# Splitting half a chunk earlier in the FFN turns, a reordered norm, and a later request for the norm's vectors

## The chip, the cores and the metric

The kernel runs on one core of a Trainium2 chip. TensorE (PE) multiplies, VectorE (DVE) and ScalarE (ACT) work beside it, GpSimd (POOL) does small work, and SyncE (SP) issues the loads from HBM in a program of its own. The metric is the device time of one execution in microseconds, lower is better: 3050.05 us before, the median of 3 runs (3048.78 to 3052.07).

## The reference

Two layers over a stream x of 256 tokens by 2048 channels, everything in float32:

```
proj = x @ w_in + b_in                       # 2048 -> 3*1024 + 512 + 512 + 3*2048
p_sb = stick_breaking_attention(q, k, v) @ sb_w_out
p_ssm = glu(gelu(s5(u))) @ ssm_w_out
p_mem = memory_attention(q_mem, mem) @ mem_w_out
merged = sum of sigmoid(gate_b) * p_b
x = layer_norm(ALPHA * x + merged @ w_o) * ln1_g + ln1_b
gate, up = split(x @ ffn_w_gate_up)          # 2048 -> 2 * 5632
x = layer_norm(ALPHA * x + (silu(gate) * up) @ ffn_w_down) * ln2_g + ln2_b
```

The change touches the first norm of each layer, the FFN behind it, and a few steps of the second norm of the first layer.

## The kernel before

**Numbers.** Each float32 operand is split into two parts: hi is a copy rounded to the type fp32r, lo is the rest. A product is hi times hi, hi times lo and lo times hi. The activations xs hold both parts of x side by side (columns 0 to 255 hi, 256 to 511 lo).

**Chunks.** All weights come in chunks of 1 MB (128 partitions by 2048) into one of 4 slots of `raw`. A chunk is split in two halves of 128x1024. For each half ACT writes the hi part (`hi_half`, L631, one ACTIVATE), and DVE subtracts it to get lo (`lo_half`, L978, one TENSOR_TENSOR). There are 4 buffers for halves, so half h of chunk c+2 can be split only when PE has finished half h of chunk c (semaphore `half_done`). The helper `split_next` at chunk c splits both halves of chunk c+1. PE waits on `lo_ready` before each half (L1481 and L1483 for gate/up, L1491 to L1493 for the rows of the down projection, L1466 and L1469 for other products).

**Each engine's instructions are written out by hand** and run in that order; between engines stand semaphores alone. An instruction that waits holds everything behind it on its engine.

**An FFN turn** has 12 chunks: 0 to 7 gate/up, two for each of four pairs of tiles (q = 0 to 3: gate, up, gate, up), 8 to 11 down. There are 11 turns in a layer: the first, nine in a loop, the last. After each odd chunk c < 8 comes the eviction of its pair: ACT waits for the whole chunk, copies the PSUM part to `pt` (L929), DVE adds (L1424, into gg or uu). For an up pair (c = 3 and c = 7) DVE then multiplies twice (L1428, L1432), ACT writes the hi of `hT` (L936) and DVE its lo (L1435). In program order the split of chunk c+1 stands before the eviction, the split of chunk c+2 after it.

**The norm** after w_o (v = 0 in layer 0, v = 2 in layer 1; `which` = 0) and the one after the FFN (`which` = 1). DVE gathers the statistics and the scale `rv` (L1037 to L1063), both engines centre the rows in five pieces (0 to 127, 128 to 511, then three of 512; DVE token half 0 at L1071, ACT half 1 at L711). PE transposes 16 slices (L1560, `turn(k)`, two instructions each), the two engines apply g and b in turn (DVE L1078 even k, ACT L718 odd k), ACT writes the hi part (L726), DVE the lo part (L1083), and PE multiplies slice k at once (`step(k)`: for `which` = 0 the first pair of the FFN, chunks 0 and 1). turn(k) for k of 4 to 7 needs the third piece centred. 16 matmuls that nobody reads, "fillers" (L1836), stand on PE between w_o and the first norm.

**Loads.** SP issues chunk after chunk; the request for a chunk waits until the lo parts of the chunk 4 before it are done (L368). The vectors ln_g and ln_b are broadcast into `gbh` in two parts of 1024 columns, 512 KB each vector (L455, `load_norm`); a request for the second part waits for `resid_done`, which DVE raises in the first FFN turn after two of four residual steps (L1115 and L1119, at c = 2 and c = 4; the other two, at c = 6 and c = 8, use the second part).

Of the kernel before, what the change touches and what calls it, by code (L numbers as in the profile page):

```python
# [19 lines left out]
KD = D // P  # L20
# [93 lines left out]
def trunk(nc, x, mem, w_in, b_in, sb_w_out, lam_re_d, lam_im_d, log_dt_d, b_re_d, b_im_d, c_re_d,  # L114
# [3 lines left out]
    with ctx:  # L118
# [234 lines left out]
        def _(sp):  # L353
# [29 lines left out]
            for l in range(DEPTH):  # L383
# [85 lines left out]

                def ffn_loads(i, first=False):  # L470
                    for c in range(8):
                        if first and c == 7:
                            load_norm(2 * l, 1)
                        load("FF", l, i, c, column_pair(w_gu[l], i * 512 + (D_FF * ((c // 2) % 2) + 256 * (c // 4)),
                                                        8 * (c % 2)))
                    for c in range(4):
                        load("FF", l, i, 8 + c, block_rows(w_down[l], bass.ds(i * 4 + 2 * (c % 2), 2),
                                                           1024 * (c // 2)))
# [144 lines left out]
        def _(act):  # L623
# [35 lines left out]
            def done(ph, l, i, c, h=1):  # L659
                return chunk_no(ph, l, i, c) * 2 + (h + 1 + HALF_CREDIT)  # L660
# [41 lines left out]
            def norm(l, which):  # L702

                v = 2 * l + which
                ph, i, c = ("U", 0, 0) if which else ("FF", 0, 0)

                def centre(q):
                    y = rows[:, 1, CENTRES[q]:CENTRES[q + 1]]
                    if q == 0:
                        act.wait_ge(ln_step, LN_STEPS * (v + 1))  # L710
                    act.activation(y, y, ACT.Identity, bias=rv[:, 4, 1:2], scale=rv[:, 1, 1:2]).then_inc(norm_act, 1)  # L711

                def affine(k):
                    g, b = norm_cols(l, which, k)
                    act.wait_ge(ln_T, 16 * v + k + 1)
                    if k >= 4:
                        act.wait_ge(xs_lo, 16 * v + k - 3)
                    act.activation(xf[:, k % 4, :], bank[k % 4][:, 0:T], ACT.Identity, bias=b, scale=g  # L718
                                   ).then_inc(aff_act, 1)

                def hi_part(k):
                    if k % 2:
                        act.wait_ge(aff_act, 8 * v + k // 2 + 1)
                    else:
                        act.wait_ge(aff_dve, 8 * v + k // 2 + 1)
                    act.activation(xs[:, k, 0:T], xf[:, k % 4, :], ACT.Copy).then_inc(xs_hi, 1)  # L726

                split_next(ph, l + which, i, c)
                centre(0)
                centre(1)  # L730
                for k in range(0, KD, 2):
                    affine(k + 1)
                    hi_part(k)
                    hi_part(k + 1)
                    if k in (0, 2, 4):
                        centre(2 + k // 2)

            for l in range(DEPTH):

# [176 lines left out]
                def ffn_turn(i, first, last):  # L916
                    n = i + 11 * l
                    for c in range(12):
                        if last and c == 11:
                            if not last_l:  # L920
                                for h in range(2):
                                    hi_half("U", l + 1, 0, 0, h)
                        elif not (first and c == 0):
                            split_next("FF", l, i, c)
                        if c < 8 and c % 2:
                            q, a = c // 2, c // 4
                            act.wait_ge(half_done, done("FF", l, i, c))
                            act.wait_ge(tile_out, tile_no("FF", l, i, q) + 1)
                            act.activation(pt[:, q % 2], banks[:, PAIR_BANK[q]:PAIR_BANK[q] + 2, 0:T], ACT.Copy  # L929
                                           ).then_inc(first_out, 1)  # L930
                            if q % 2 == 0:
                                act.wait_ge(tile_out, tile_no("FF", l, i, q) + (1 + TILE_CREDIT))
                                act.activation(th[:], gg[:], ACT.Tanh, scale=0.5).then_inc(ffn_th, 1)
                            else:
                                act.wait_ge(ffn_step, n * 4 + (2 * a + 2 + 2))
                                act.activation(hT[:, 2 * a:2 * a + 2, 0:T], hh[:], ACT.Copy).then_inc(ffn_hi, 1)  # L936
# [17 lines left out]
        def _(dve):  # L954
# [70 lines left out]
            def norm(l, which):  # L1025
                v = 2 * l + which
                base = LN_STEPS * v
                k = [0]
# [57 lines left out]
                def split(h):  # L1086
                    lo_half(PHASES[nxt[0]][1][nxt[3]], hl_slot(ph, c + 1, h), h,
                            chunk_no(ph, l + which, i, c) * 2 + (2 + h))

                centre(0)  # L1090
                centre(1)
                affine(0)
# [3 lines left out]
                for k in range(2, KD, 2):  # L1096
                    affine(k)
                    lo_part(k - 2)
                    lo_part(k - 1)
                    if k < 6:  # L1100
                        centre(2 + k // 2)
                    if k == 4 and not which:
                        split(0)
                    if k == 8:
                        split(1)
                lo_part(KD - 2)
                lo_part(KD - 1)

            def residual(v, q):

# [41 lines left out]
            for l in range(DEPTH):  # L1152
# [245 lines left out]

                def ffn_turn(i, first, last):
                    n = i + 11 * l  # L1400
                    for c in range(12):
                        if last and c == 11:
                            if not last_l:
                                for h in range(2):
                                    lo_half(PHASES["U"][1][0], h, h, chunk_no("U", l + 1, 0, 0) * 2 + h)
                        elif not (first and c == 0) and not (last and c == 10):
                            split_next("FF", l, i, c)
                        if last and c == 9:
                            row = [(m, 0, banks[:, 4 + 2 * m:6 + 2 * m, :],
# [9 lines left out]
                        if c < 8 and c % 2:  # L1419
                            q, a = c // 2, c // 4  # L1420
                            src = banks[:, PAIR_BANK[q]:PAIR_BANK[q] + 2, T:2 * T]
                            dve.wait_ge(ffn_step, n * 4 + (2 * a + 1 + q % 2))
                            dve.wait_ge(first_out, tile_no("FF", l, i, q) + 1)
                            dve.tensor_tensor((gg, uu)[q % 2][:], pt[:, q % 2], src, ALU.add).then_inc(tile_out, 1)  # L1424
# [33 lines left out]
        def _(pe):  # L1458
# [88 lines left out]
            def norm(l, which, step):  # L1547
# [16 lines left out]
                for k in range(4):  # L1564
                    turn(k)
                for k in range(KD):
                    if k + 4 < KD:
                        turn(k + 4)
                    pe.wait_ge(xs_lo, 16 * v + k + 1)
                    step(k)  # L1570

            for l in range(DEPTH):

# [258 lines left out]
                    pair_k("FF", l, 0, k // 8, k, PAIR_BANK[0], k == KD - 1)  # L1832

                pe.wait_ge(rows_out, sums_no("WO", l, 1, 0))
                for k in range(16):
                    pe.matmul(bank[0], ident_r[:], xs[:, k, :], start=True, stop=True)  # L1836
                norm(l, 0, first_pair)
                for q in range(1, 4):
                    ffn_pair(0, q)
# [52 lines left out]
```

## Time and profile before

| | us |
|---|---|
| median of 3 runs | 3050.05 |
| the profiled execution, its time | 3046.98 |
| its span | 3045.2 |
| PE busy | 2973.9 (98%) |
| DVE busy | 2055.1 (67%) |
| ACT busy | 1455.0 (48%) |
| mean share of the DMA engines on the weight queue | 59.3% |

PE is busy almost always. The other engines have room on average, so what costs time are the places where PE waits for one of them at that moment. "Busy" is drawn a little long for PE: matmuls overlap, and the row of one reaches beyond the start of the next.

### The profile page before, as it was taken

What the parts mean: (1) busy time and instruction counts of PE and PEld (TensorE: products, weight loads), DVE (VectorE), ACT (ScalarE), POOL (GpSimd) and SP (SyncE); (2) the same over time, 40 slices, a digit from 0 to 9 for tenths busy, and PEclk for the clock granted to TensorE, in tenths of its full rate; (3) what the DMA queues carried; (4) which work ended last, traced back from release to release, by engine and by line L of the source; (5) the groups of instructions that cost most, each with busy time, mean ns of one, the idle gap of its engine ahead of it and who ended that gap; (6) DMA issues with size and microseconds to landing.
All of it is one profiled execution on the core that took longest, in us unless ns stands there. A gap on an engine that the chain in (4) does not pass through costs nothing.

```text
span 3045.2 us, 46770 instructions
## 1 busy us (share of the span) xinstructions
PE 2973.9 (98%) x16206; PEld 2538.1 (83%) x16206; DVE 2055.1 (67%) x3163; ACT 1455.0 (48%) x1975; POOL 130.2 (4%) x191
## 2 busy tenths in 40 slices
PE   6999999999999999999999999999999999999999
PEld 5888888888788888888878888888878888888887
DVE  5999766665765555555699996666667556555656
ACT  4556555554444444444455655555444444444443
POOL 5000011110000000000000000000000000000000
PEclk8999999999999999999999999999999999999999
DMA  8656577675555555555465656767755555555554
GB/s 276 164 155 170 153 193 192 180 206 207 202 186 192 193 191 179 181 193 191 161 161 159 163 158 180 200 174 197 231 177 180 193 184 174 192 193 180 190 183 151
DMA packets 672969, 562.16 MB, mean 185 GB/s; under 512 B 20760, under 2 KB 637568, under 8 KB 671872
## 3 DMA queue, kind: packets, MB, share of 16 engines
q1 hardware_dynamic: 668688, 548.48, 59.3%
q10 hardware_dynamic: 4208, 12.74, 1.1%
q8 instruction: 43, 0.70, 0.1%
q14 instruction: 30, 0.25, 0.0%
HBM read 552.78 MB, written 8.39 MB: 184 GB/s over the span
## 4 chain that ended last, share of the span: by engine, by line
PE 82%; DVE 10%; ACT 3%; issue 3%; POOL 1%; DMA 1%; ACTq 1%; DVEq 0%; POOLq 0%
PE banks L1466 21%; PE banks L1481 19%; PE banks L1469 11%; PE banks L1483 9%; PE banks L1491 6%; PE banks L1493 5%; PE banks L1492 5%; DVE lo L978 3%; PE banks L1757 2%; ACT hi L631 2%; DVE hh L1432 1%; DVE hh L1428 1%; PE banks L1759 1%; ACT pt L929 1%; DVE st L1139 1%
## 5 line engine op out<-in xcount | busy, mean ns | idle before, releaser
L978 DVE TENSOR_TENSOR lo<-raw,hi 128x1024 fp32r<-128x1024 f32 x1016 | 1214.5, 1238 | 262.6 <-ACT hi L631 230.5
L631 ACT ACTIVATE hi<-raw 128x1024 fp32r<-128x1024 f32 x884 | 890.0, 1051 | 352.2 <-PE banks L1493 235.9
L1481 PE MATMUL banks<-xs,hi 128*128 128x512 f32 x2816 | 892.1, 398 | 10.9 <-DVE lo L978 10.5
L1466 PE MATMUL banks<-xs,hi 128*128 128x512 f32 x2544 | 807.0, 399 | 6.0 <-DVE lo L978 4.7
L1483 PEld LDWEIGHTS banks<-xs,lo 128*128 128x128 f32 x2816 | 530.7, 188 | 125.4
L1469 PEld LDWEIGHTS banks<-xs,lo 128*128 128x128 f32 x2544 | 478.7, 188 | 113.2
L1483 PE MATMUL banks<-xs,lo 128*128 128x256 f32 x2816 | 555.0, 279 | 0.0
L1469 PE MATMUL banks<-xs,lo 128*128 128x256 f32 x2544 | 500.9, 278 | 0.0
L1481 PEld LDWEIGHTS banks<-xs,hi 128*128 128x128 f32 x2816 | 432.0, 189 | 17.6 <-DVE lo L978 16.0
L1466 PEld LDWEIGHTS banks<-xs,hi 128*128 128x128 f32 x2544 | 388.7, 189 | 14.0 <-issue 7.4
L1491 PE MATMUL banks<-hi,hT 128*128 128x512 f32 x704 | 276.4, 393 | 8.4 <-DVE lo L978 8.4
L1492 PE MATMUL banks<-lo,hT 128*128 128x512 f32 x704 | 274.2, 389 | 0.0
L1493 PE MATMUL banks<-hi,hT 128*128 128x512 f32 x704 | 274.1, 389 | 0.0
L929 ACT ACTIVATE pt<-banks 128x512 f32<-128x512 f32 x88 | 52.8, 600 | 387.0 <-PE banks L1483 387.0
L656 ACT ACTIVATE tmp<-banks,par 128x256 f32<-128x256 f32 x144 | 68.4, 475 | 326.8 <-PE banks L1469 326.8
L1128 DVE TENSOR_TENSOR rows<-rows,banks 128x1024 f32<-128x1024 f32 (+1 forms) x98 | 109.5, 1152 | 108.7 <-PE banks L1493 108.6
L643 ACT ACTIVATE hi<-raw 128x1024 fp32r<-128x1024 f32 x132 | 134.8, 1052 | 79.6 <-PE banks L1493 79.6
L1491 PEld LDWEIGHTS banks<-hi,hT 128*128 128x128 f32 x704 | 132.1, 188 | 43.7 <-DVE lo L978 14.8
L1493 PEld LDWEIGHTS banks<-hi,hT 128*128 128x128 f32 x704 | 132.1, 188 | 27.8
L1492 PEld LDWEIGHTS banks<-lo,hT 128*128 128x128 f32 x704 | 132.2, 188 | 26.0
L1424 DVE TENSOR_TENSOR uu<-pt,banks 128x512 f32<-128x512 f32 x44 | 30.3, 688 | 165.2 <-ACT pt L929 165.2
L1424 DVE TENSOR_TENSOR gg<-pt,banks 128x512 f32<-128x512 f32 x44 | 30.3, 688 | 144.6 <-ACT pt L929 144.6
(216 smaller groups left out, 2683.3 us busy)
## 6 DMA issues: line engine op xcount, KB each, us to landing
raw<-in_ffn_w_gate_up SPq DMA_DIRECT2D x176, 1024.0 KB, 5.1
raw<-in_w_in SPq DMA_DIRECT2D x160, 1024.0 KB, 7.6
raw<-in_ffn_w_down SPq DMA_DIRECT2D x88, 1024.0 KB, 5.2
raw<-in_w_o SPq DMA_DIRECT2D x32, 1024.0 KB, 5.3
raw<-in_mem_w_kv SPq DMA_DIRECT2D x16, 1024.0 KB, 5.5
raw<-in_sb_w_out SPq DMA_DIRECT2D x32, 512.0 KB, 4.1
raw<-in_ssm_w_out SPq DMA_DIRECT2D x32, 256.0 KB, 4.4
raw<-in_mem_w_out SPq DMA_DIRECT2D x32, 256.0 KB, 4.8
```

The costliest lines, as they stand in the source:

```text
L631: act.activation(hi[:, hl_slot(ph, c, h), :], raw[:, slot, h * HALF:(h + 1) * HALF], ACT.Copy).then_inc(hi_ready, 1)
L643: act.activation(hi[:, hl_slot(ph, c + 1, h), :], raw[:, slot, h * HALF:(h + 1) * HALF], ACT.Copy).then_inc(hi_ready, 1)
L929: act.activation(pt[:, q % 2], banks[:, PAIR_BANK[q]:PAIR_BANK[q] + 2, 0:T], ACT.Copy).then_inc(first_out, 1)
L978: dve.tensor_tensor(lo[:, s, :], raw[:, slot, h * HALF:(h + 1) * HALF], hi[:, s, :].bitcast(F32), ALU.subtract).then_inc(lo_ready, 1)
L1128: dve.tensor_tensor(y2, y2, src, ALU.add).then_inc(rows_out, 1)
L1466: pe.matmul(dst[:, :], hi[:, s, k * P:(k + 1) * P], x_t[:, k0 + k, :], start=first and k == 0, stop=False)
L1469: ins = pe.matmul(dst[:, 0:T], lo[:, s, k * P:(k + 1) * P], x_t[:, k0 + k, 0:T], start=False, stop=last and k == 7)
L1481: pe.matmul(bank[base + j], hi[:, s, at[j]], xs[:, k, :], start=k == 0, stop=False)
L1483: ins = pe.matmul(bank[base + j][:, 0:T], lo[:, s, at[j]], xs[:, k, 0:T], start=False, stop=last)
L1491: pe.matmul(dst, xh, hi[:, s, w], start=first, stop=False)
L1492: pe.matmul(dst, xh, lo[:, s, w], start=False, stop=False)
L1493: return pe.matmul(dst, xl, hi[:, s, w], start=False, stop=last)
```

## The change

1. In an FFN turn, half 0 of chunk c+2 is split ahead of the eviction after c = 1, 3, 5, 7; half 1 follows in the next step of the loop (c in 2, 4, 6, 8).
2. In the first norm of a layer ACT also splits chunk 2, half 0 after slice 10 and half 1 after slice 14, and DVE follows (`second_pair`). So the first turn doesn't split chunk 2 any more.
3. ACT in both norms: the third piece is centred and the hi part of slice 0 written before ACT's first `affine`.
4. PE in the first norm: 24 fillers for 16, and turn(4) behind step(0).
5. SP: ln_g and ln_b, second part, are requested behind gate/up chunk 7 of the first turn, not ahead of it.

```diff
@@ ffn_loads
                     for c in range(8):
-                        if first and c == 7:
-                            load_norm(2 * l, 1)
                         load("FF", l, i, c, column_pair(...))
+                    if first:
+                        load_norm(2 * l, 1)
@@ norm, scalar
                 centre(0)
                 centre(1)
+                centre(2)
+                hi_part(0)
                 for k in range(0, KD, 2):
                     affine(k + 1)
-                    hi_part(k)
+                    if k:
+                        hi_part(k)
                     hi_part(k + 1)
-                    if k in (0, 2, 4):
+                    if k in (2, 4):
                         centre(2 + k // 2)
+                    if k in (10, 14) and not which:
+                        hi_half("FF", l, 0, 2, (k - 10) // 4)
@@ ffn_turn, scalar (vector: the same with lo_ahead)
-                        elif not (first and c == 0):
+                        elif c in (2, 4, 6, 8):
+                            hi_half("FF", l, i, c + 1, 1)
+                        elif not (first and c < 2):
                             split_next("FF", l, i, c)
                         if c < 8 and c % 2:
                             q, a = c // 2, c // 4
+                            hi_half("FF", l, i, c + 2, 0)
                             act.wait_ge(half_done, done("FF", l, i, c))
@@ norm, vector
+                    if k == 12 and not which:
+                        second_pair(0)
                 lo_part(KD - 2)
                 lo_part(KD - 1)
+                if not which:
+                    second_pair(1)
@@ norm, tensor
                 for k in range(KD):
-                    if k + 4 < KD:
+                    if k + 4 < KD and (k or which):
                         turn(k + 4)
                     pe.wait_ge(xs_lo, 16 * v + k + 1)
                     step(k)
+                    if k == 0 and not which:
+                        turn(4)
@@ tensor, fillers
-                for k in range(16):
-                    pe.matmul(bank[0], ident_r[:], xs[:, k, :], start=True, stop=True)
+                for k in range(24):
+                    pe.matmul(bank[0], ident_r[:], xs[:, k % KD, :], start=True, stop=True)
```

ScalarE in the loop over FFN turns, from chunk 2's split to the eviction of the up pair. The kernel before (`hi` a half's hi part, `pt` the copy from PSUM, `hT` the hi part of the down projection's input, raw_full the arrival of a chunk in slot 0 to 3):

```order
L929 ACTIVATE pt<-banks 128x512 [waits tile_out]
L932 REGISTER_ALU
L933 ACTIVATE th<-gg 128x512 [waits tile_out]
L629 REGISTER_ALU
L630 ISA [waits raw_full3]
L631 ACTIVATE hi<-raw 128x1024 [waits half_done]
L630 REGISTER_ALU
L631 ACTIVATE hi<-raw 128x1024 [waits half_done]
L629 REGISTER_ALU
L630 ISA [waits raw_full0]
L631 ACTIVATE hi<-raw 128x1024 [waits half_done]
```

The changed kernel, at the same place:

```order
L630 ISA [waits raw_full3]
L631 ACTIVATE hi<-raw 128x1024 [waits half_done]
L935 REGISTER_ALU
L936 ISA [waits half_done]
L937 ACTIVATE pt<-banks 128x512 [waits tile_out]
L940 REGISTER_ALU
L941 ACTIVATE th<-gg 128x512 [waits tile_out]
L630 REGISTER_ALU
L631 ACTIVATE hi<-raw 128x1024 [waits half_done]
L629 REGISTER_ALU
L630 ISA [waits raw_full0]
```

The wait for chunk 3's arrival and its first hi part moved from behind `pt` and `th` to ahead of them; the second hi part stayed behind. The same happens at c = 3, 5 and 7, and on DVE.

PE at the start of the first norm, before (`ident_r` marks the fillers, `ident,rows` a transpose, `xs,hi` and `xs,lo` a step):

```order
L1836 MATMUL banks<-xs,ident_r 128x512 x15
L1560 MATMUL banks<-ident,rows 128x128 [waits norm_act,norm_done]
...
L1560 MATMUL banks<-ident,rows 128x128 [waits aff_dve,norm_act,norm_done]
L1560 MATMUL banks<-ident,rows 128x128
L1481 MATMUL banks<-xs,hi 128x512 [waits lo_ready,rows_out,xs_lo]
L1481 MATMUL banks<-xs,hi 128x512
L1483 MATMUL banks<-xs,lo 128x256 x2
```

And now:

```order
L1860 MATMUL banks<-xs,ident_r 128x512 x23
L1582 MATMUL banks<-ident,rows 128x128 [waits norm_act,norm_done]
...
L1503 MATMUL banks<-xs,hi 128x512 [waits lo_ready,rows_out,xs_lo]
L1503 MATMUL banks<-xs,hi 128x512
L1505 MATMUL banks<-xs,lo 128x256 x2
L1582 MATMUL banks<-ident,rows 128x128 [waits aff_dve,norm_act,norm_done]
L1582 MATMUL banks<-ident,rows 128x128
```

Eight fillers more, and the transpose that waits for DVE's first `affine` and for the third centred piece moved behind the first step.

SP in the first FFN turn, before (the end of w_o, seven gate/up chunks, the vectors, the eighth chunk, the down chunks):

```order
L368 DMA raw<-in_w_o 128x2x1024 [waits lo_ready] x5
L368 DMA raw<-in_ffn_w_gate_up 128x8x256 [waits lo_ready] x7
L455 DMA gbh<-in_ln_g 128x1024 [waits resid_done]
L455 DMA gbh<-in_ln_b 128x1024
L368 DMA raw<-in_ffn_w_gate_up 128x8x256 [waits lo_ready]
L368 DMA raw<-in_ffn_w_down 128x2x1024 [waits lo_ready] x4
```

And now, the same stretch of SP:

```order
L368 DMA raw<-in_w_o 128x2x1024 [waits lo_ready] x5
L368 DMA raw<-in_ffn_w_gate_up 128x8x256 [waits lo_ready] x8
L455 DMA gbh<-in_ln_g 128x1024 [waits resid_done]
L455 DMA gbh<-in_ln_b 128x1024
L368 DMA raw<-in_ffn_w_down 128x2x1024 [waits lo_ready] x4
```

The wait for `resid_done` now holds back the four down chunks and not the eighth gate/up chunk.

## Rows read from the trace of the kernel before

**Rows 1.** The page's first line.
```profile
span 3045.2 us, 46770 instructions
```
**Rows 2.** PE's waits, whole run: engine line waited for: us in total, times, longest us.
```profile
PE banks L1481 <- DVE lo L978: 10.5, 20, 3.4
PE banks L1491 <- DVE lo L978: 10.0, 24, 0.8
```
**Rows 3.** Timeline, PE, chunk 5 of a loop turn: start, us, line, xcount, [idle before <-releaser].
```profile
1223.82 0.62 PE L1481 MATMUL banks<-xs,hi 128*128 128x512 f32 x2
1224.51 0.63 PE L1481 MATMUL banks<-xs,hi 128*128 128x512 f32 x2
...
1225.58 0.73 PE L1481 MATMUL banks<-xs,hi 128*128 128x512 f32 x2 [0.21 <-DVE lo L978]
```
**Rows 4.** Timeline, ACT and DVE, the same place.
```profile
1219.91 0.60 ACT L929 ACTIVATE pt<-banks 128x512 f32<-128x512 f32 x1 [4.59 <-PE banks L1483]
...
1224.30 4.63 DVE L978 TENSOR_TENSOR lo<-raw,hi 128x1024 fp32r<-128x1024 f32 x4 [0.26 <-ACT hi L631]
```
**Rows 5.** Timeline, chunk 9 of the same turn: the eviction on ACT, then PE.
```profile
1242.69 0.60 ACT L929 ACTIVATE pt<-banks 128x512 f32<-128x512 f32 x1 [4.59 <-PE banks L1483]
...
1248.43 0.50 PE L1491 MATMUL banks<-hi,hT 128*128 128x512 f32 x1 [0.40 <-DVE lo L978]
```
**Rows 6.** Timeline, first turn of layer 0: PE at chunks 7 and 9.
```profile
831.68 0.50 PE L1481 MATMUL banks<-xs,hi 128*128 128x512 f32 x1 [3.36 <-DVE lo L978]
...
843.28 0.47 PE L1491 MATMUL banks<-hi,hT 128*128 128x512 f32 x1 [0.30 <-DVE lo L978]
```
**Rows 7.** Timeline, first turn of layer 0: DVE, SP and ACT around the vectors' request.
```profile
803.13 2.36 DVE L978 TENSOR_TENSOR lo<-raw,hi 128x1024 fp32r<-128x1024 f32 x2 [1.65 <-ACT hi L631]
...
820.41 0.34 SPq L455 DMA_DIRECT2D gbh<-in_ln_g  x1
...
821.27 0.43 SPq L368 DMA_DIRECT2D raw<-in_ffn_w_gate_up  x1
...
829.31 2.00 ACT L631 ACTIVATE hi<-raw 128x1024 fp32r<-128x1024 f32 x2 [4.47 <-DMA raw<-in_ffn_w_gate_up]
```
**Rows 8.** Timeline, PE, first norm of layer 0.
```profile
774.09 3.89 PE L1836 MATMUL banks<-xs,ident_r 128*128 128x512 f32 x16
780.07 0.41 PE L1560 MATMUL banks<-ident,rows 128*128 128x128 f32 x2 [2.09 <-ACT rows L711]
...
783.41 1.20 PE L1481 MATMUL banks<-xs,hi 128*128 128x512 f32 x2
...
789.62 0.71 PE L1481 MATMUL banks<-xs,hi 128*128 128x512 f32 x2
...
799.80 0.73 PE L1481 MATMUL banks<-xs,hi 128*128 128x512 f32 x2
```
**Rows 9.** Stretches: us, PE, PEld, DVE, ACT, POOL busy, granted clock, DMA share, GB/s.
```profile
782.00:783.00 1.00, 0.00 (x0) 0.00 (x0) 0.98 (x3) 1.00 (x3) 0.00 (x0) 0.54 1.14 492
...
1543.00:1544.00 1.00, 0.00 (x0) 0.00 (x0) 1.00 (x3) 1.00 (x4) 0.00 (x0) 1.00 0.00 0
```
**Rows 10.** Timeline, DVE and ACT, first norm of layer 0.
```profile
782.02 0.76 DVE L1083 TENSOR_TENSOR xs<-xf,xs 128x256 fp32r<-128x256 f32 x2
...
782.20 0.80 ACT L711 ACTIVATE rows<-rows,rv 128x512 f32<-128x512 f32 x1
```
**Rows 11.** Timeline, PE, second norm of layer 0: last product before, first and last step.
```profile
1540.13 0.39 PE L1469 MATMUL banks<-mT,lo 128*128 128x256 f32 x2
...
1544.57 0.50 PE L1587 MATMUL banks<-xs,hi 128*128 128x512 f32 x1
...
1555.24 0.28 PE L1588 MATMUL banks<-xs,lo 128*128 128x256 f32 x1
```
**Rows 12.** SP in a loop turn: chunk 9's request; time to landing, requests of 1214 to 1240.
```profile
1226.83 0.37 SPq L368 DMA_DIRECT2D raw<-in_ffn_w_down  x1
...
DMA to landing us min/median/max: 5.0/5.2/6.5
```

More of the change, by code:

```diff
@@ L1088, in split, with second_pair @@
                             chunk_no(ph, l + which, i, c) * 2 + (2 + h))
+                def second_pair(h):
+                    lo_half(PHASES["FF"][1][2], hl_slot("FF", 2, h), h, chunk_no("FF", l, 0, 2) * 2 + h)
                 centre(0)
@@ L1400, in ffn_turn, with lo_ahead @@
                     n = i + 11 * l
+                    def lo_ahead(c, h):
+                        lo_half(PHASES["FF"][1][c], hl_slot("FF", c, h), h, chunk_no("FF", l, i, c) * 2 + h)
                     for c in range(12):
@@ L1405, in ffn_turn @@
                                     lo_half(PHASES["U"][1][0], h, h, chunk_no("U", l + 1, 0, 0) * 2 + h)
-                        elif not (first and c == 0) and not (last and c == 10):
+                        elif c in (2, 4, 6, 8):
+                            lo_ahead(c + 1, 1)
+                        elif not (first and c < 2) and not (last and c == 10):
                             split_next("FF", l, i, c)
@@ L1421, in ffn_turn @@
                             src = banks[:, PAIR_BANK[q]:PAIR_BANK[q] + 2, T:2 * T]
+                            lo_ahead(c + 2, 0)
                             dve.wait_ge(ffn_step, n * 4 + (2 * a + 1 + q % 2))
```

## The prediction

> **What bounds the kernel now.** First the page: the span is 3045.2 us [rows 1] and PE is busy 98% of it, so a gain can only come from what PE still waits for, or from steps it does at half clock. So the second view is PE's waits over the whole run [rows 2]. Two lines matter to this change: gate/up matmuls waited for a lo part 20 times, 10.5 us in all, one wait of 3.4 us; down matmuls 24 times, 10.0 us. The third view is the timeline at such places, to see the chain that ends late.
>
> In a turn of the loop PE comes to chunk 5 at 1225.58. A pair of matmuls and its partner take 0.69 to 0.70 us (1223.82 to 1224.51), so without a wait it would have come at 1225.21: 0.37 us are lost, of which the view shows 0.21 as idle, since each row is drawn some 0.16 us beyond the next start [rows 3]. What it waited for: the eviction begins at 1219.91, five steps on ACT and DVE follow, and only then does DVE start chunk 5's first lo part at 1224.30, ending 1225.5 [rows 4]. It was late for one reason: its hi part stands behind the eviction in ACT's order, though its buffer was free half a chunk before. At chunk 9 the same, after the eviction that begins at 1242.69: 0.40 idle and the same 0.16, so 0.56 us [rows 5].
>
> In the first turn of a layer PE waits 3.36 us at chunk 7 (3.52 lost) and 0.30 at chunk 9 (0.46 lost) [rows 6]. The first is a load: chunk 3's lo parts were done at 805.5, from then on chunk 7 could have been requested, but SP stood at the request for ln_g, which waits for the second residual step on DVE; it left at 820.41, chunk 7 at 821.27, and ACT got it at 829.31 after waiting 4.47 us [rows 7].
>
> In the first norm PE has its fillers at 774.09, then waits 2.09 us for the first transpose at 780.07; the first step comes at 783.41, the fifth at 789.62, chunk 2 at 799.80 [rows 8]. Four steps in 6.21 us are slow: the granted clock fell within 782 to 783 (0.54 in that stretch), the lower of its two levels, 1.2 GHz [rows 9]. From 789.62 on, eight steps with a transpose and four without (0.70 each) take 10.18 us, so one with a transpose takes 0.92.
>
> **The change part by part.** *A half ahead of the eviction.* hi of chunk c+2, half 0, needs PE to be through chunk c, half 0, which is 2.8 us before the eviction can begin. So hi (1.06) and lo (1.23) are ready about when the eviction starts, over 5 us before PE needs them. Nothing is added: the same ACTIVATE and TENSOR_TENSOR, elsewhere. What is late next is half 1. It stays behind the eviction, but moves into half 0's place: its lo ends at 1225.5 instead of 1226.7, and PE needs it at 1225.21 + 2.79 = 1228.0, so 2.5 us are left. For chunk 9 likewise: 1248.4 against 1247.9 + 2.7, 2.2 us left. The ahead split adds a wait on ACT: for the arrival of chunk c+2, with the eviction queued behind it. Chunk 9 is the tightest: requested at 1226.83, landing 5.0 to 6.5 us later [rows 12], by 1233.3; ACT turns to it 2.8 us ahead of the eviction, at about 1239.8. So I count all of it gone. Nine loop turns in two layers: 18 x (0.37 + 0.56) = 16.7 us. First and last turn of each layer, chunk 9 alone: 4 x 0.46 = 1.8 (the last turn taken as the first). Their chunk 5 shows no wait in the view; up to 1.1 more may hide there, which I leave out.
>
> *The vectors behind chunk 7.* Its request moves from 821.27 to about 805.5, lands by 812 and is needed at 828. 2 x 3.52 = 7.0 us. What is now behind SP's wait are the four down chunks. Chunk 8 used to come fourth behind the two vectors and chunk 7; now it takes chunk 7's place, on ACT at 829.3 at the latest, lo at 831.6, and PE wants it at 828.2 + 5.6 = 833.7: 2.1 us are left, more since the second residual step now stands behind one lo part and not two. The residual steps that use the vectors get them no later.
>
> *The norm.* Fillers: 16 take 3.73 us to the next start, 24 take 5.6 and end at 779.7; the transposes start at 780.07 whatever they do, so they cost nothing, with 0.4 us to spare. First step: it needed turn(4), which waited for ACT's third centred piece, 782.20 to 783.0; it now needs only slice 0's lo part. DVE's first two ran from 782.02, the first ends at 782.4 [rows 10]. hi of slice 0 can't be later than before: its input is ready at 781.1 and the centred piece takes about 0.5. So the first step comes at 782.45, 0.95 us earlier. The clock: in the second norm PE's last full product ended at 1540.4 and the first step came at 1544.57, 4.2 us with only transposes between [rows 11], and the granted clock stayed 1.00 [rows 9]. In the first norm it was 777.8 to 783.41, 5.6 us, and it fell. With 24 fillers and the earlier step it is 779.7 to 782.45, 2.8 us. So I take the upper level, 2.4 GHz: 12 x 0.92 + 4 x 0.70 = 13.8 us from 782.45, chunk 2 at 796.3, 3.5 us gained if PE alone sets the pace.
>
> The Trainium skill, "TensorE: Matmul & The Clock Gate", Part 4: PE-mode transpose, says that a transpose doesn't count as PE being busy in the way a matmul does. That speaks against counting only the idle pieces (0.4 and 0.95 us) as quiet, and it is why I compare the whole stretches; by either count the changed norm is quieter for less time than the second norm, which kept its clock. It raises my chance of a fall from 3 to 8 in 100, and doesn't change the sum.
>
> DVE and ACT have to keep up. In the second norm, paced by them, 16 steps took 1544.57 to about 1555.4, 10.8 us [rows 11]; chunk 2's first lo part adds 1.2. 12.0 is under 13.8, so in total they can, but the split halves (1.2 us each) stand between slices and will make single steps late. Bounds per norm: 3.5 (none late) and 1.0 (clock falls: 0.95, little else). I take 2.6, nearer to the upper one since the sum of DVE's work fits. 2 x 2.6 = 5.2. The reordering in the second norm I count at nothing: DVE sets the pace there, and its order is as before.
>
> Sum: 16.7 + 1.8 + 7.0 + 5.2 = 30.7 us. The profiled execution took 3046.98 us (span 3045.2), so 3016.3 there; the median before, 3050.05, lies 3.1 above it. Predicted on that scale: 3019.3 us.
>
> **The rivals.** *The clock falls all the same.* For it: idle pieces remain. Against: the second norm. Each norm gains 1.0: 3022.5 us.
>
> *Half 1 takes the place of half 0.* For it: the eviction's chain is as long as before. Against: 2.2 to 2.5 us of margin. If half of the gain of the turns came back: 3019.3 + 9 = 3028 us.
>
> *The down chunks are late in the first turn.* They now queue behind the vectors; in the first turn before, queued requests took 8 us to arrive. Margin 2.1 us; if it is missed by as much as chunk 7 was, the 7.0 us return at chunk 8: 3026 us.
>
> *Slower than before: ACT holds the eviction for a load.* The place is c = 7 of each turn, hi of chunk 9 ahead of `pt`. If the landing took over some 16 us from 1226.83, the eviction would start late; its chain takes 4.1 us (1219.91 to 1224.04, where DVE's idle 0.26 begins [rows 4]), so it ends at 1246.8, and PE needs hT's second pair at 1247.9, so it decides from about 17 us on. At 20 us it would cost 3 us a turn, 66 us for 22 turns against 31 gained: 3085 us. Against it: 6.5 us is the longest landing in that stretch.
>
> *Nothing gained:* the waits only move to other places of the turn, 3050 us. The period of PE's work leaves no place I can name.
>
> **How the numbers follow.** Forecast 75 in 100, clock 8, half 1 5, down chunks 7, slower 3, nothing gained 2. The forecast's own range: the norm term from 1.0 to 3.5 each, the hidden 1.1, and some 2 us of spread of a median give 3014 to 3025. Holding the down chunks' and half 1's cases too, 3013 to 3028. Faster by over 0.2% (6 us, what a measurement of this kernel can tell): 0.95; within it 0.02; slower 0.03.
>
> **What would show it.** PE's waits: gate/up behind a lo part down from 20 to at most a few and none of 3 us; down matmuls behind a lo part without the 22 of the turns. A loop turn, 67.5 us before, takes 66.6. Clock 1.00 through the first norms, first step 2.8 us after the fillers, chunk 2 some 22.2 us after their start (25.7 before). Chunk 7 requested before the vectors. Wrong would make it: an ACT wait for a DMA inside the turns, a stretch at 0.50 clock in a first norm, a new PE wait at chunk 8, or steps of the norm more than 1.5 us behind slices from DVE.

## The result, and the profile after

3011.98 us, the median of 4 runs (3008.55 to 3012.73), against 3051.06 us (3048.78 to 3053.14, 4 runs). The ratio is 0.987, with a 95% interval of 0.9858 to 0.9882: 39.1 us faster. Forecast were 30.7 us and a range whose fast end was 3013 us. The direction was right, the size was too small by a fifth of the measured gain, and the time lies 1.0 us below the range. The profiled execution took 3008.55 us against 3046.98, so 38.4 us can be taken apart in the traces.

The page's first line, and PE's waits over the whole run (line waited for: us in total, times, longest us):

```profile
span 3006.8 us, 46802 instructions
```
```profile
PE banks L1488 <- DVE lo L986: 8.8, 7, 2.1
...
PE banks L1503 <- DVE xs L1091: 2.9, 4, 0.8
...
PE banks L1513 <- DVE lo L986: 1.5, 2, 0.8
```

Gate/up matmuls (L1503) no longer wait for a lo part at all, down matmuls (L1513) twice and outside the FFN turns [rows 2]. In their place stand four waits of a norm's step for DVE, 2.9 us; L1488 is other products, as before.

Chunk 5 of a loop turn, timeline of PE in the changed kernel:

```profile
1209.90 0.63 PE L1503 MATMUL banks<-xs,hi 128*128 128x512 f32 x2
1210.37 0.39 PE L1505 MATMUL banks<-xs,lo 128*128 128x256 f32 x2
1210.60 0.62 PE L1503 MATMUL banks<-xs,hi 128*128 128x512 f32 x2
1211.07 0.40 PE L1505 MATMUL banks<-xs,lo 128*128 128x256 f32 x2
```

The boundary at 1210.60 can't be told from any other [rows 3]. The same place, ACT and DVE:

```profile
1202.44 1.06 ACT L631 ACTIVATE hi<-raw 128x1024 fp32r<-128x1024 f32 x1 [1.73 <-PE banks L1505]
1203.53 1.23 DVE L986 TENSOR_TENSOR lo<-raw,hi 128x1024 fp32r<-128x1024 f32 x1 [1.56 <-ACT hi L631]
1205.31 0.60 ACT L937 ACTIVATE pt<-banks 128x512 f32<-128x512 f32 x1 [1.80 <-PE banks L1505]
...
1209.69 3.50 DVE L986 TENSOR_TENSOR lo<-raw,hi 128x1024 fp32r<-128x1024 f32 x3 [0.26 <-ACT hi L631]
```

Half 0's lo part is done at 1204.8, before the eviction (`pt`) starts and 5.8 us before PE needs it at 1210.60; half 1's is done at 1210.9, 2.5 us before PE needs it. That is as forecast [rows 4].

The first turn of layer 0: SP and ACT (chunk 7 is the second of the two requests of the first row; the down chunks come behind the vectors).

```profile
795.75 4.98 SPq L368 DMA_DIRECT2D raw<-in_ffn_w_gate_up  x2
815.15 0.34 SPq L455 DMA_DIRECT2D gbh<-in_ln_g  x1
...
816.01 1.78 SPq L368 DMA_DIRECT2D raw<-in_ffn_w_down  x3
```
```profile
824.35 2.01 ACT L631 ACTIVATE hi<-raw 128x1024 fp32r<-128x1024 f32 x2 [3.07 <-DMA raw<-in_ffn_w_down]
826.90 1.06 ACT L631 ACTIVATE hi<-raw 128x1024 fp32r<-128x1024 f32 x1 [0.54 <-DMA raw<-in_ffn_w_down]
829.43 0.60 ACT L937 ACTIVATE pt<-banks 128x512 f32<-128x512 f32 x1 [1.47 <-PE banks L1505]
```

Chunk 7 is requested over 14 us ahead of the vectors, and nobody waits for it [rows 7]. ACT does wait for chunk 8 now, 3.07 us, and for chunk 9 ahead of an eviction, 0.54 us; but it then waits for PE once more (1.47 us before `pt`), so neither costs anything.

The first norm of layer 0, PE, and the granted clock (us, PE, PEld, DVE, ACT, POOL busy, clock, DMA share, GB/s):

```profile
778.43 0.41 PE L1582 MATMUL banks<-ident,rows 128*128 128x128 f32 x2 [0.23 <-ACT rows L711]
...
780.72 0.72 PE L1503 MATMUL banks<-xs,hi 128*128 128x512 f32 x2 [0.85 <-DVE xs L1091]
...
784.60 0.38 PE L1582 MATMUL banks<-ident,rows 128*128 128x128 f32 x2
785.59 0.73 PE L1503 MATMUL banks<-xs,hi 128*128 128x512 f32 x2 [0.61 <-DVE xs L1091]
```
```profile
780.00:781.00 1.00, 0.28 (x1) 0.28 (x2) 0.84 (x3) 0.97 (x3) 0.00 (x0) 1.00 1.21 524
781.00:782.00 1.00, 1.00 (x9) 0.92 (x9) 0.77 (x3) 1.00 (x4) 0.00 (x0) 1.00 1.14 492
```

The fillers start at 772.44, so the first step comes after 8.3 us (9.3 before) [rows 8]. The end of the norm is measured below by the first eviction (ACT's first `pt`), which waits for the last step: it begins 23.55 us after the fillers' start, 25.77 before. PE starts chunk 2 close to it, 0.20 us ahead of it here and 0.06 us before the change. The clock stays at 1.00 [rows 9]. But the fifth step, at 785.59, waits for DVE.

Where the 38.4 us lie, from starts of the same instruction in both traces:

| term | forecast | measured | how measured |
|---|---|---|---|
| 18 loop turns | 16.7 | 21.3 | 67.52 to 66.34 us a turn |
| two first turns | 0.9 + 7.0 | 9.7 | 71.26 to 66.45 and 71.33 to 66.43, first eviction to first eviction |
| two last turns | 0.9 | 1.9 | 0.39 + 0.56 each |
| two first norms | 5.2 | 4.4 | fillers to the first eviction, 25.77 to 23.55 and 25.72 to 23.54 |
| all else | 0 | 1.1 | fillers of layer 0 start 1.65 earlier; 0.55 lost between the layers |

The last row can't be put down to the change: in the 14 profiled executions of this study the fillers of layer 0 started anywhere from 772.4 to 776.0 us, and the stretch from the last down matmul of layer 0 to the fillers of layer 1 took 734.6 to 736.2 us with the old as with the new order of the norms. The norm's row has some luck in it too: in the eight first norms profiled with the old norm and 16 fillers (two in each of four executions), the first eviction came 24.8 to 26.1 us after the fillers' start.

### The profile page after: what moved, and what is told of

Read it like the earlier page. It is cut to its first block, busy times and chain, and to the rows that moved or that the text cites. A ratio compares the mean times of both kernels' runs of the same rounds, so it can differ in the third digit from the quotient of the medians.

```text
span 3006.8 us, 46802 instructions
## 1 busy us (share of the span) xinstructions
PE 2958.4 (98%) x16222; PEld 2536.1 (84%) x16222; DVE 2062.7 (69%) x3163; ACT 1468.9 (49%) x1975; POOL 129.8 (4%) x191
## 4 chain that ended last, share of the span: by engine, by line
PE 92%; DVE 5%; POOL 1%; ACT 1%; issue 1%; ACTq 0%; DMA 0%; DVEq 0%; POOLq 0%
PE banks L1488 22%; PE banks L1503 22%; PE banks L1491 11%; PE banks L1505 11%; PE banks L1513 7%; PE banks L1514 7%; PE banks L1515 7%; PE banks L1781 2%; DVE lo L986 1%; PE banks L1783 1%; DVE st L1154 1%; DVE scan_t L1230 0%; DVE rows L1143 0%; DVE blocks L1238 0%; POOL sc L317 0%
## 5 line engine op out<-in xcount | busy, mean ns | idle before, releaser
L631 ACT ACTIVATE hi<-raw 128x1024 fp32r<-128x1024 f32 x884 | 904.9, 1053 | 542.1 <-PE banks L1505 288.0
L1503 PE MATMUL banks<-xs,hi 128*128 128x512 f32 x2816 | 886.4, 396 | 2.9 <-DVE xs L1091 2.9
L1488 PE MATMUL banks<-xs,hi 128*128 128x512 f32 x2544 | 807.6, 399 | 6.6 <-DVE lo L986 4.7
L1503 PEld LDWEIGHTS banks<-xs,hi 128*128 128x128 f32 x2816 | 430.0, 189 | 5.7 <-DVE xs L1091 3.9
L1488 PEld LDWEIGHTS banks<-xs,hi 128*128 128x128 f32 x2544 | 388.9, 189 | 14.6 <-issue 8.2
L1513 PE MATMUL banks<-hi,hT 128*128 128x512 f32 x704 | 274.0, 389 | 0.0
L643 ACT ACTIVATE hi<-raw 128x1024 fp32r<-128x1024 f32 x132 | 134.8, 1052 | 79.6 <-PE banks L1515 79.6
L1513 PEld LDWEIGHTS banks<-hi,hT 128*128 128x128 f32 x704 | 132.1, 188 | 26.7
L999 DVE SCALAR_TENSOR_TENSOR gate<-banks,tmp 128x256 f32<-128x256 f32 x96 | 40.8, 425 | 126.6 <-ACT tmp L656 126.6
L1513 PE MATMUL banks<-hi,mT 128*128 128x512 f32 x256 | 99.9, 390 | 1.5 <-DVE lo L986 1.5
```

The lines of the kernel that those rows point to most:

```text
L631: act.activation(hi[:, hl_slot(ph, c, h), :], raw[:, slot, h * HALF:(h + 1) * HALF], ACT.Copy).then_inc(hi_ready, 1)
L643: act.activation(hi[:, hl_slot(ph, c + 1, h), :], raw[:, slot, h * HALF:(h + 1) * HALF], ACT.Copy).then_inc(hi_ready, 1)
L1488: pe.matmul(dst[:, :], hi[:, s, k * P:(k + 1) * P], x_t[:, k0 + k, :], start=first and k == 0, stop=False)
L1503: pe.matmul(bank[base + j], hi[:, s, at[j]], xs[:, k, :], start=k == 0, stop=False)
L1513: pe.matmul(dst, xh, hi[:, s, w], start=first, stop=False)
```

## The experiments

Times are compared with the kernel before on the same chip. The time of a turn is that from an eviction to the same one nine turns later, by nine. Spreads of a median are some 2 us, traces agree to 0.02 us in the turns, so mechanisms are read from the traces.

**Only the half ahead in the turns** (`turns_only`): the turns' part of the diff on the kernel before, chunk 2 still split by the first turn. ScalarE's edits (VectorE's are the same, with `lo_ahead`):

```diff
+                        elif c in (2, 4, 6, 8):
+                            hi_half("FF", l, i, c + 1, 1)
                         elif not (first and c == 0):
                             split_next("FF", l, i, c)
                         if c < 8 and c % 2:
                             q, a = c // 2, c // 4
+                            hi_half("FF", l, i, c + 2, 0)
```

> Only the turns' half ahead of each eviction, on the kernel before. Theory (a wait costs its gap and then 0.11 us more in the first matmuls behind it, which the prediction left out): a loop turn of 67.53 us becomes 66.35, 18 of them give 21.2 us; first and last turns give some 4 and 1.9 more, since the second residual step also comes one lo part earlier and with it chunk 7's request: about 27 us faster than before. Rival (the gap alone, 0.93 a turn; the rest of the surplus is from other parts of the change): 66.60 a turn, about 21 us.

3023.27 us against 3050.68, ratio 0.9913 (0.9896 to 0.9929), 27.4 us. A loop turn took 66.337 us in both layers: all of the 1.18 us come from this part, 0.25 more than the visible gaps. The first turn did not behave as expected: from first eviction to first eviction it took 70.83 and 70.78 us in the two layers, 1.0 us less in all where some 4 were expected. SP asked for the vectors 1.6 us earlier, counted from the first eviction, but ACT met chunk 7 at another place:

```profile
827.41 1.06 ACT L631 ACTIVATE hi<-raw 128x1024 fp32r<-128x1024 f32 x1 [10.37 <-DMA raw<-in_ffn_w_gate_up]
828.38 0.58 ACT L932 ACTIVATE pt<-banks 128x512 f32<-128x512 f32 x1
```

With half 0 ahead, the late chunk holds the eviction as well: the stall moves one eviction forward. First to fourth eviction take 36.94 us against 37.69 in layer 0, but 37.76 against 37.73 in layer 1. PE's wait at chunk 7 was of about one length in both, 2.70 and 2.65 us. In layer 0 the clock stayed at 1.00 and two short waits followed behind the late eviction (0.39 and 0.56 us); in layer 1 the clock fell to 0.50 and those two were absent. This is the slower rival's mechanism, in the one place where a load is late enough. It also makes the forecast time partly luck: the traces account for 24.8 us (span 3045.2 to 3020.4), of which 24.2 lie in the turns, and the other 2.6 of the 27.4 are explained by nothing in them.

**Only the later request** (`load_only`).

```diff
-                        if first and c == 7:
-                            load_norm(2 * l, 1)
+                    if first:
+                        load_norm(2 * l, 1)
```

> Only the later request for ln_g and ln_b, on the kernel before. Theory: PE's wait at chunk 7 of each first turn goes, 3.52 + 0.11 each, 7.3 us, and no new wait at chunk 8. Rival (the down chunks are late instead): a new wait at chunk 8 of up to 3.5 us, near 0 gained.

3040.88 us against 3050.68, ratio 0.9965 (0.9952 to 0.9977), 9.8 us, more than the 7.3 expected. In the trace first to fourth eviction take 34.09 us against 37.69, 3.6 a layer as expected, and PE has no wait at chunk 8. The next run suggests why the time gains more.

**Only 24 fillers** (`fill24_only`).

```diff
-                for k in range(16):
-                    pe.matmul(bank[0], ident_r[:], xs[:, k, :], start=True, stop=True)
+                for k in range(24):
+                    pe.matmul(bank[0], ident_r[:], xs[:, k % KD, :], start=True, stop=True)
```

> Only 24 fillers for 16, on the kernel before. Theory (the clock falls when too little happens on PE between the fillers' end and the first step): the stretch without matmuls of full width shrinks from 5.6 to 3.8 us, the clock stays at 1.00, four steps take 3.7 and not 6.2 us, 2 x 2.4 = 4.8 us faster. Rival (the reordering is what kept the clock): it falls as before, 0 us.

3047.10 us against 3050.68; the interval of the ratio, 0.9982 to 1.0002, contains no change. The norm gained what the theory says: clock 1.00, first eviction 23.36 us after the fillers' start in both layers, 2.4 a layer. But most of it was given back some 30 us later, at the wait for chunk 7 (columns as above):

```profile
782.00:783.00 1.00, 0.00 (x0) 0.00 (x0) 0.96 (x4) 1.00 (x3) 0.00 (x0) 1.00 1.21 524
828.00:829.00 1.00, 0.00 (x0) 0.00 (x0) 0.70 (x1) 1.00 (x2) 0.00 (x0) 1.00 1.04 414
829.00:830.00 1.00, 0.41 (x1) 0.42 (x2) 1.00 (x2) 0.43 (x2) 0.00 (x0) 0.55 1.03 414
830.00:831.00 1.00, 1.00 (x4) 0.81 (x4) 1.00 (x2) 1.00 (x2) 0.00 (x0) 0.50 1.01 401
```

After waits of 3.42 and 4.48 us the granted clock fell to the lower level, and the part from the third to the fourth eviction took 16.15 and 17.19 us, against 14.77 and 14.80: 3.8 us given back of the 4.8 gained. Of layer 1's 2.4 us, 1.1 are the longer wait itself, so the fall costs 1.3 us in either layer. In the profiled execution of the kernel before the clock stayed at 1.00 behind the same wait of 3.36 us, in both layers. So this wait costs 3.6 us, and 1.3 more where the clock falls. That it fell in both layers in most unprofiled runs of the kernel before would explain the surplus of `load_only` (7.2 + 2.6 = 9.8 us). It is not shown: of those runs only the mean granted clock is recorded, 0.992 to 0.994, which is too coarse to tell.

**ScalarE alone ahead** (`after_act_ahead`): the changed kernel, DVE makes both lo parts behind the eviction.

```diff
                         elif c in (2, 4, 6, 8):
+                            lo_ahead(c + 1, 0)
                             lo_ahead(c + 1, 1)
...
-                            lo_ahead(c + 2, 0)
```

> The changed kernel, but in the turns only ScalarE splits a half ahead; VectorE makes both lo parts behind the eviction. VectorE then starts chunk 5's lo right after hT's lo, 0.2 us earlier than in the kernel before. Theory (gap + 0.11 each): gaps of 0.17 and 0.36, a loop turn of 66.35 + 0.28 + 0.47 = 67.10 us, 15 us slower than the changed kernel over 20 turns. Rival (gap alone): 66.88 us a turn, 11 us slower.

3020.07 us against 3050.68, ratio 0.9903 (0.9887 to 0.9920). A turn took 66.831 us, 0.49 more than 66.337. By that figure alone the rival came nearer, but the expected 0.75 and 0.53 both rested on gaps that I had put too long. The trace gives the real ones (timeline of PE at chunk 5, then at chunk 9):

```profile
1147.04 0.39 PE L1505 MATMUL banks<-xs,lo 128*128 128x256 f32 x2
1147.29 0.73 PE L1503 MATMUL banks<-xs,hi 128*128 128x512 f32 x2
1147.86 0.40 PE L1505 MATMUL banks<-xs,lo 128*128 128x256 f32 x2
...
1169.35 0.39 PE L1515 MATMUL banks<-hi,hT 128*128 128x512 f32 x1
1169.79 0.50 PE L1513 MATMUL banks<-hi,hT 128*128 128x512 f32 x1
1170.13 0.39 PE L1514 MATMUL banks<-lo,hT 128*128 128x512 f32 x1
```

Chunk 5 starts 0.25 behind its neighbour where 0.23 is usual, a gap of 0.02. But the pair that starts there takes 0.57 to the next start and not 0.47. At chunk 9 the gap is 0.44 - 0.23 = 0.21, and the next start comes after 0.34 instead of 0.23. Gaps alone make 0.23 a turn; with 0.10 and 0.11 behind them 0.44, near the 0.49 measured. With the true gaps the theory holds and the rival falls: even a wait of 0.02 us costs 0.12.

**A longer eviction chain** (`before_long_chain`, `after_long_chain`): on the kernel before and on the changed one.

```diff
+                                act.activation(tmp[:], hh[:], ACT.Copy)
                                 act.activation(hT[:, 2 * a:2 * a + 2, 0:T], hh[:], ACT.Copy).then_inc(ffn_hi, 1)
```

> The kernel before with one more ScalarE copy of 128x512 (0.53 us, nobody reads it) in each up pair's eviction. Theory (gap plus a fixed 0.11): both gaps of a loop turn grow by 0.53, the matmul behind them still takes 0.11 more than the others, the turn takes 67.52 + 1.06 = 68.58 us. Rival (the extra grows with the wait): the surplus doubles, over 68.7 us.

> The changed kernel with the same extra copy. Theory (half 1 has 2.2 to 2.5 us to spare): the loop turn stays at 66.34 us. Rival (half 1 is nearly late, the change has no room): it grows, up to 67.4.

On the kernel before a turn took 68.556 us, 1.04 more (3075.57 us, one run). PE at chunk 5:

```profile
1166.35 0.39 PE L1484 MATMUL banks<-xs,lo 128*128 128x256 f32 x2
1167.46 0.73 PE L1482 MATMUL banks<-xs,hi 128*128 128x512 f32 x2 [0.72 <-DVE lo L979]
1168.03 0.40 PE L1484 MATMUL banks<-xs,lo 128*128 128x256 f32 x2
```

The gap is 0.88 now, and the pair behind it takes the same 0.57. With gaps of 0.02, 0.37 and 0.88 us the surplus behind them was 0.10 each time: it is fixed. The run's time rose by 23.6 us, more than the turns explain, since the clock fell at the wait for chunk 7 in both layers here (waits of 3.53 and 3.42 us). On the changed kernel the turn took 66.337 us to the last digit (3010.61 us, one run): half 1 has at least the 0.53 us to spare, as forecast.

**The norm's parts**, four edits of the changed kernel, one kernel each. `after_fill16` and `after_fill32`, other numbers of fillers:

```diff
-                for k in range(24):
+                for k in range(16):
```
```diff
-                for k in range(24):
+                for k in range(32):
```

`after_norm_order`, the old order on ScalarE and on PE:

```diff
-                centre(2)
-                hi_part(0)
...
-                    if k:
-                        hi_part(k)
+                    hi_part(k)
...
-                    if k in (2, 4):
+                    if k in (0, 2, 4):
...
-                    if k + 4 < KD and (k or which):
+                    if k + 4 < KD:
...
-                    if k == 0 and not which:
-                        turn(4)
```

`after_late_split`, VectorE's split of chunk 1, half 0, one pair of slices later:

```diff
-                    if k == 4 and not which:
+                    if k == 6 and not which:
```

> The changed kernel with 16 fillers. Theory (the fillers keep the clock, not the reordering): the stretch without full-width matmuls is 3.7 to 8.3 us after the fillers' start, 4.6 us; the clock falls in the first norms, chunk 2 starts 25 to 26 us after the fillers' start instead of 23.55, 4 us slower in all. Rival (the earlier first step is enough): clock 1.00, 23.55, no change.

> The changed kernel with the old order of the norm on ScalarE and of turn(4) on PE; fillers 24, chunk 2's split still inside. Theory (VectorE's split between slices sets the pace, the earlier first step is given back): chunk 2 at 23.3 to 23.6 us after the fillers' start, as now, no difference in the time. Rival (the prediction's account: 0.95 us a norm from the earlier first step): 24.4 us, 2 us slower.

> The changed kernel, VectorE splits chunk 1's half 0 after slice 5's lo part and not after slice 3's. Theory (that split is what makes a step of the norm late by 0.77 us): the wait goes, chunk 2 comes about 22.8 us after the fillers' start instead of 23.55, 1.5 us faster in all, too little for the time alone. Rival (VectorE's work is as much, a later step is late instead): 23.5.

> The changed kernel with 32 fillers. Theory (fillers are free up to the first transpose at 5.98 us after their start): they end at 7.5 us, the first step comes 1.5 us later, chunk 2 at about 25.0 us, 3 us slower in all. Rival (there is slack behind the transposes): chunk 2 at 23.6.

| kernel | us (before on that chip) | clock | first step | first eviction |
|---|---|---|---|---|
| before | 3051.06 | falls | 9.32 | 25.77 |
| the change | 3010.04 (3050.39) | 1.00 | 8.27 | 23.56 |
| after_fill16 | 3011.82 (3052.01) | falls | 8.27 | 25.2 |
| after_norm_order | 3009.54 (3052.01) | 1.00 | 9.17 | 23.48 |
| after_late_split | 3010.66 (3050.39) | 1.00 | 8.26 | 23.10 |
| after_fill32 | 3012.16 (3050.39, one run) | 1.00 | 9.73 | 25.0 |

The last two columns are us from the fillers' start, layer 0; layer 1 differs by at most 0.05. The times of the last five rows lie within 2.6 us of each other and tell nothing apart; the traces do. Without the eight fillers the clock falls in spite of the earlier first step. The fillers ended at 777.5, from then on PE ran only the transposes, the granted clock was 0.96 in the stretch from 780 and 0.50 in the next, and the first step came at 782.02, at the lower level. Some 1.65 us a norm are lost:

```profile
780.00:781.00 1.00, 0.81 (x8) 0.64 (x6) 0.82 (x2) 1.00 (x3) 0.00 (x0) 0.96 1.21 524
781.00:782.00 1.00, 0.30 (x2) 0.00 (x0) 0.97 (x3) 0.97 (x3) 0.00 (x0) 0.50 1.06 459
```

Without the reordering, the first eviction comes 0.07 us earlier than with it. The first step's gain of 0.9 us is given back in full: the wait at the fifth step (the PE row at 785.59 in the trace of the changed kernel) is 0.61 us, with the overlap of 0.16 that rows of PE are drawn with 0.77. Later by one pair of slices, DVE's split costs 0.46 us less; the rest of the wait came back at other steps, so the result (23.10) lies between the theory (22.8) and its rival (23.5). And fillers beyond the first transpose cost one for one: 32 of them make the transposes 1.49 us late and the first eviction 1.45.

```profile
773.56 7.63 PE L1860 MATMUL banks<-xs,ident_r 128*128 128x512 f32 x32
781.03 1.03 PE L1582 MATMUL banks<-ident,rows 128*128 128x128 f32 x8
```

**The changed kernel with the vectors ahead of chunk 7** (`after_old_load`), **and the changed kernel again** (`after_again`).

```diff
+                        if first and c == 7:
+                            load_norm(2 * l, 1)
...
-                    if first:
-                        load_norm(2 * l, 1)
```

> The changed kernel with the vectors requested ahead of chunk 7 again. Theory (PE's wait of 3.5 us is the load's, and it can let the clock fall): chunk 7's arrival now holds ScalarE ahead of an eviction, each first turn is 3.5 us longer, in all 7 us slower, and up to 1.4 more for each layer in which the granted clock falls there. Rival (the earlier second residual step hides the load): 5 us or less.

> The changed kernel itself on this chip, to compare the others with: 3009 to 3013 us, loop turn 66.34 us, chunk 2 at 23.55 us after the fillers' start.

3019.87 us against 3010.04 on the same chip: 9.8 us. First to fourth eviction take 37.93 and 39.04 us instead of 33.44, 10.1 us in all. PE (timeline) and the clock (columns as above):

```profile
825.20 0.40 PE L1505 MATMUL banks<-xs,lo 128*128 128x256 f32 x2
828.26 0.73 PE L1503 MATMUL banks<-xs,hi 128*128 128x512 f32 x2 [2.66 <-DVE lo L986]
```
```profile
829.00:830.00 1.00, 1.00 (x7) 0.91 (x7) 0.00 (x0) 1.00 (x2) 0.00 (x0) 0.76 1.02 406
830.00:831.00 1.00, 1.00 (x4) 0.81 (x4) 0.55 (x1) 1.00 (x2) 0.00 (x0) 0.50 1.03 414
```

The wait returns at chunk 7, 2.66 us in layer 0 and 3.77 in layer 1, with no second one behind the late eviction, and the clock falls behind it in both layers. Taking off the start that PE missed and 0.1 for what follows a wait, the fall costs 1.7 us a layer. The rival, that the earlier residual step hides the load, is wrong. No version here beats the changed kernel by more than the times can tell.

## Why the prediction was right and wrong

**What bounds the kernel, and where it waits: right.** The waits named went, and no other came in their place in the turns. Half 1 had the room forecast for it. Chunk 8's first lo part was done 2.5 us before PE wanted it, for 2.1 forecast. Chunk 9 arrived in time except for 0.54 us that nobody felt. The prediction named an ACT wait for a DMA inside the turns as a sign of being wrong; there are two in each first turn, and they cost nothing.

**The size of a wait: wrong, and it is the term that made the forecast miss.** The step said: 0.37 and 0.56 us lost at chunks 5 and 9, from the start that PE missed. What was measured is 0.48 and 0.70. `after_act_ahead` and `before_long_chain` show the difference: the first matmuls behind a wait take 0.10 to 0.11 us more than others, whatever the wait's length, and this was in the row that I quoted [rows 3]: its pair is drawn 0.73 long and the one before it 0.63. I corrected the idle time for the overlap of rows and did not look at the next start. The 18 loop turns give 4.6 us of the 7.7 missing: 3.8 are this surplus behind 36 waits, and 0.04 us a turn, 0.8 in all, stay unexplained.

The trace shows where the 0.1 us may come from. The weight loads (PEld) of chunk 5's first two pairs in the kernel before:

```profile
1225.58 0.30 PEld L1481 LDWEIGHTS banks<-xs,hi 128*128 128x128 f32 x2 [0.41 <-DVE lo L978]
1225.58 0.73 PE L1481 MATMUL banks<-xs,hi 128*128 128x512 f32 x2 [0.21 <-DVE lo L978]
...
1226.27 0.31 PEld L1481 LDWEIGHTS banks<-xs,hi 128*128 128x128 f32 x2
1226.38 0.64 PE L1481 MATMUL banks<-xs,hi 128*128 128x512 f32 x2
```

The second pair's load starts 0.11 us ahead of its matmul; behind the wait both start at once. A lost lead of 0.11 us would be the surplus, and it would be the same whatever the length of the wait. Steps of a norm that follow a transpose without any wait fit this: at 786.53 in the changed kernel the load starts only 0.02 us ahead, and the pair takes 0.55 us to the next start. No run moved the load by itself, so this reading is argued, not shown; the size of the surplus is shown.

**First and last turns: too small by 1.8 and 1.0 us.** I left out their chunk 5, where the view of waits marks nothing, and said that up to 1.1 might hide there. It was 0.26 to 0.27 in gaps for each of four places and 0.1 behind each. In the first turn of the kernel before, chunk 5 starts at 816.90 where 816.63 was due:

```profile
816.40 0.39 PE L1483 MATMUL banks<-xs,lo 128*128 128x256 f32 x2
816.90 0.73 PE L1481 MATMUL banks<-xs,hi 128*128 128x512 f32 x2
```

A view that marks no wait shows no short one either: it subtracts the 0.16 us of overlap and drops the rest. The waits at chunks 7 and 9 had their 0.1 as well, and so had a wait of 0.14 at the start of chunk 2 in each first turn ([rows 8], the row at 799.80), which the prediction did not count.

**The vectors behind chunk 7: right in the mechanism,** 3.6 us a layer for 3.52. Not seen was that the clock can fall behind the wait; where it does, as in both layers of `after_old_load`, the later request is worth 9.8 us in the time.

**The norm: 4.4 for 5.2, for half of the reasons.** The clock stayed up, as forecast from the second norm, and `after_fill16` shows that the fillers do it. The 0.95 us of the earlier first step were counted as gained, less 0.9 for late steps; in fact the reordering is worth nothing (`after_norm_order`), and what was measured is the clock's 2.4 less 0.1 for the split of chunk 2 and less 0.1 for the reordering. That 4.4 lies near 5.2 is partly luck. The bound of 1.0 us "if the clock falls" was nearer to 0.6.

**Transposes and the clock.** In `after_fill16`, with eight transposes between 5.98 and 7.5 us after the fillers' start, the clock was at 0.96 in the stretch that holds most of them and at 0.50 in the next, before the first step could come. The changed kernel, with the same transposes after 24 fillers, kept it. The Trainium skill, "TensorE: Matmul & The Clock Gate", Part 4: PE-mode transpose, says that a transpose doesn't count as PE being busy in the way a matmul does. The trace is in keeping with it, but PE was also idle for 2.09 us before these transposes, and no run takes the two apart.

**The rest, 1.1 us,** is the start of the program, which varies from execution to execution.

The range was too narrow at its fast end: it was built from bounds of the norm, the hidden 1.1 us and 2 us of spread, with no bound for the per-wait cost. The turns alone had 44 waits at chunks 5 and 9.

## What to carry to other kernels

Price a short wait by when the next few instructions start, not by the idle time or the first start alone: here a fixed 0.1 us came on top, and the 36 waits of 0.37 and 0.56 us in the loop turns were worth a quarter more than they looked. A half-step moved ahead of an eviction is free as long as its input is surely there; where a load can be late, the eviction is late with it, so move the load's request first. When an engine's first step of a paced chain comes earlier, look for the step at which the pacing engine falls behind; the fillers here did best when they ended just before the work that they bridge to.

## What was not expected of the hardware

The surplus behind a wait was 0.10 to 0.11 us for waits of 0.02, 0.21, 0.37, 0.56 and 0.88 us.

The length of the wait at chunk 7 did not tell whether the granted clock fell behind it. Ten such waits were profiled. It fell behind both in `fill24_only` (3.42 and 4.48 us), in `before_long_chain` (3.53 and 3.42) and in `after_old_load` (2.66 and 3.77). In `turns_only` it fell behind the wait of 2.65 us and not behind the one of 2.70. In the kernel before it fell behind neither of two waits of 3.36 us. What decides it stays open. A fall cost 1.3 to 1.7 us where it could be told from the wait.
